# Decode attention: key pages turned in 32x32 blocks by VectorE and scored by TensorE in small tiles, values requested after the last gather

## The chip, the cores and the metric

One Trainium2 chip, one core of it. The metric is the device time of one launch in microseconds (us). The kernel before was run three times: 1145.11, 1141.04 and 1144.10 us, median 1144.1 us.

## What is computed

One layer of a decoder with a prompt group (256 tokens) and a sample group: 8 samples with 8 new tokens each and 2,048 past tokens in pages of 128. Cut to what the change touches, per sample:

```python
# MoBA: 8 heads, keys and values in paged cache [k, v]; top 3 blocks of 256 keys by mean key, plus the own block
gate = einsum('bthd,bnhd->bthn', q, kmean);  _, top = top_k(gate, 3)
# NSA: 8 query heads on 2 key heads; cache rows [k_cmp, v_cmp, k_sel, v_sel]
ck = gelu(flat(k_cmp) @ w1 + b1) @ w2 + b2        # 127 compressed keys, 32 rows each, stride 16; the same for v_cmp
p_cmp = softmax(q @ ck.T);  imp = p_cmp @ overlap  # importance of 64-row blocks
_, idx = top_k(imp, 16)                            # selected blocks, attended over k_sel, v_sel
o_win = attention over the last 512 rows (k_win, v_win)
```

All of it is float32. Ahead of the samples stand the input projections and the prompt's attention, behind them the mixers' projections and the feed-forward layer.

## The kernel before, in words

Four blocks follow each other: `front_block`, `prompt_block`, `decode_block` and `back_block`. The samples are done in `decode_block`: a prologue for sample 0, then a loop of 7 passes, in which the engines finish sample `it` while the segments of sample `it + 1` are prepared, and the last sample apart. In the trace the passes of the loop begin at 288.7, 348.8, 408.9 us and so on, the last sample at 708.9 us, and the back at 751 us. The order of each engine's work is written by hand (`sequence` of each engine); the PSUM banks that pass data from TensorE to VectorE and ScalarE are taken in turn from a ring of four (`RING`, the list `STEADY` of jobs), and TensorE may fill a bank when the job four places ahead in the list has been emptied (`wait_emptied`, L1162).

TensorE's pass (`sequence`, L1345) has two parts.

- From the key scores to the selected probabilities. `key_transposes` (L1225) turns the key pages of a quarter (4 of the 16 pages of 128 rows x 512) with 16 transposes of 128x128; ScalarE and VectorE copy each full bank to `KTr` (`key_copy`, L1491). `key_scores` (L1234) multiplies a quarter: 4 matmuls of 32 query columns by 512 keys. VectorE takes each quarter with a sum, a masked add and a maximum (`take_keys`, L1679). Between them stand `hidden_values` (L1261), 48 products of 128x128x128 for the compressed values, the own, window and compressed scores, and the importance (L1371). VectorE ranks the blocks (L1724 to L1745) and ScalarE takes the exponential of the selected scores (L1544); only then TensorE transposes the selected probabilities (job `psel`, L1386), the first job that needs them.
- From the probabilities to the next sample's segments. `segments(q)` transposes the compressed rows of a quarter that ScalarE has relaid (`relay_quarter`, L1521); `moba_values` (L1268) multiplies probabilities and values; `selected_transposes` (L1185) turns the selected keys and `selected_scores` (L1192) multiplies them for two quarters (a pair); `hidden_keys` (L1210) makes 12 products per quarter for the compressed keys; `compressed_values` (L1325), `compressed_products` (L1335) and `final_transposes` (L1293) finish sample `it`.

The NSA rows of a quarter come by an indirect DMA of POOL (`gather_segments`, L551) into one of two slots; `slot_free` (L1147) waits for the slot's copies and for the selected transposes of that quarter:

```python
pool.wait_ge(filled, nth(b - 1 if b else None, ("sel", q, 0)))
```

SyncE (`sequence`, L1107) requests key and value pages. Kr holds 8 key pages, so two quarters of keys are requested in the first part of the pass, and two for the next sample behind them. The next sample's values are requested as soon as `moba_values` has used a slot:

```python
for q in (1, 2, 0):
    sp.wait_ge(v_used, it * 4 + (q + 1 if q else 4))
    load_v(it + 1, q)
```

`prompt_block` begins on SyncE with 8 loads of the prompt's own NSA rows (L608).

## Time and profile before

| what | us |
|---|---|
| three runs, median | 1144.1 |
| profiled execution, its span (the page gives no other time of it) | 1140.6 |
| one pass of the loop (408.9 to 468.9 us) | 60.0 |
| TensorE busy over the span | 1051.8 |
| VectorE busy over the span | 528.8 |
| ScalarE busy over the span | 544.4 |

The page's busy time is an average over blocks with different limits. The change touches the decode loop, so that one pass of it is read: 408 to 468 us, the third of seven passes of the same length. Idle time of an engine stands in brackets before an instruction, with what ended it.

### The profile page before, as it was taken

Reading aid. Unit: us, or ns where it says so; the run is one execution under the profiler, and the core shown is the slowest. Engines: PE = TensorE matmul, PEld = TensorE weight load, DVE = VectorE, ACT = ScalarE, POOL = GpSimd, SP = SyncE. Lnnn points to the kernel's source line nnn. Section 1 sums busy time; section 2 is a strip of 40 time slices with the busy share of each in tenths; the row PEclk is TensorE's granted clock in tenths of the full one; section 3 lists DMA queues with packets and bytes.
Section 4 is the critical chain, followed back from the end, with each engine's and each line's share of the span. In section 5 each row is a group of like instructions: output and inputs, shape, how many; then the busy total and the mean of one; then the engine's idle time right before and its main releaser. Section 6 shows DMA issues by size and latency. Waiting matters only on the chain. (4 is left out here: it accounts for less than half of the span.)

```text
span 1140.6 us, 25588 instructions
## 1 busy us (share of the span) xinstructions
PE 1051.8 (92%) x9297; PEld 912.2 (80%) x9297; DVE 528.8 (46%) x1174; ACT 544.4 (48%) x1069; POOL 83.0 (7%) x59
## 2 busy tenths in 40 slices
PE   7789996867999999999999999989999799999997
PEld 3578874656777787778787878769998799999997
DVE  1500015524545545463637363657457755555324
ACT  3422214645575666565756564561543444443223
POOL 1143410001000000000000100000000000000000
PEclk9799995867999999999999999988999899999999
DMA  9797776407666575758484846593565154443501
GB/s 331 214 309 246 246 255 224 178 37 279 221 212 231 193 242 179 269 159 284 134 305 132 310 147 221 182 268 103 176 201 166 41 181 147 147 147 148 185 0 47
DMA packets 129909, 219.51 MB, mean 192 GB/s; under 512 B 19348, under 2 KB 74129, under 8 KB 125058
## 3 DMA queue, kind: packets, MB, share of 16 engines
q1 hardware_dynamic: 124962, 185.14, 49.2%
q0 software_dynamic: 4896, 33.68, 8.0%
q8 instruction: 34, 0.56, 0.2%
q14 instruction: 17, 0.14, 0.0%
HBM read 210.46 MB, written 12.45 MB: 195 GB/s over the span
## 5 line engine op out<-in xcount | busy, mean ns | idle before, releaser
L103 PE MATMUL ps<-b_uH,b_slabH 128*128 128x320 f32 x480 | 152.3, 317 | 8.8 <-DVE b_uL L2341 5.3
L104 PE MATMUL ps<-b_uL,b_slabH 128*128 128x320 f32 x480 | 151.7, 316 | 0.0
L105 PE MATMUL ps<-b_uH,b_slabL 128*128 128x320 f32 x480 | 151.0, 315 | 0.0
L1207 PE MATMUL ps<-t_XT,t_slab 128*128 128x128 f32 x1024 | 142.6, 279 | 4.6 <-DVE t_XT L1655 3.5
L2229 DVE TENSOR_TENSOR b_slabL<-t_slab,b_slabH 128x2048 fp32r<-128x2048 f32 (+1 forms) x52 | 109.3, 2124 | 65.2 <-ACT b_slabH L2122 65.2
L1207 PEld LDWEIGHTS ps<-t_XT,t_slab 128*128 128x128 f32 x1024 | 127.2, 193 | 14.8 <-issue 10.6
L2122 ACT ACTIVATE b_slabH<-t_slab 128x2048 fp32r<-128x2048 f32 (+1 forms) x52 | 92.3, 1783 | 96.0 <-PE ps L105 90.6
L103 PEld LDWEIGHTS ps<-b_uH,b_slabH 128*128 128x128 f32 x480 | 93.4, 195 | 10.3 <-issue 6.6
L1504 ACT ACTIVATE t_KTr<-ps 128x512 f32<-128x512 f32 x152 | 82.1, 592 | 23.4 <-PE ps L1231 19.9
L104 PEld LDWEIGHTS ps<-b_uL,b_slabH 128*128 128x128 f32 x480 | 93.3, 194 | 0.0
L105 PEld LDWEIGHTS ps<-b_uH,b_slabL 128*128 128x128 f32 x480 | 93.1, 194 | 0.0
L1207 PE MATMUL ps<-t_XT,t_taps 128*128 128x128 f32 x512 | 83.9, 279 | 0.0
L1231 PEld LDWEIGHTS ps<-t_ident,t_Kr 128*128 128x128 f32 x512 | 55.7, 141 | 20.1 <-issue 13.2
L1207 PEld LDWEIGHTS ps<-t_XT,t_taps 128*128 128x128 f32 x512 | 69.5, 192 | 2.1 <-issue 1.4
L551 POOL DMA_INDIRECT t_nsa<-cache_nsa_kv,t_index x32 | 30.1, 941 | 509.8 <-ACT t_vsel L1504 293.0
L1231 PE MATMUL ps<-t_ident,t_Kr 128*128 128x128 f32 x512 | 62.4, 275 | 0.1
L1654 DVE TENSOR_TENSOR t_XT<-ps,t_XT 128x256 f32<-128x256 f32 x64 | 26.9, 420 | 75.6 <-PE ps L1182 50.5
L1504 ACT ACTIVATE t_relay<-t_nsa 128x512 f32<-128x512 f32 x64 | 36.7, 620 | 38.1 <-DMA t_nsa<-cache_nsa_kv,t_index 37.9
L103 PE MATMUL ps<-b_GH,b_slabH 128*128 (+1 forms) x176 | 54.5, 310 | 0.0
L105 PE MATMUL ps<-b_GH,b_slabL 128*128 (+1 forms) x176 | 54.4, 309 | 0.0
L104 PE MATMUL ps<-b_GL,b_slabH 128*128 (+1 forms) x176 | 54.4, 309 | 0.0
L237 POOL TENSOR_TENSOR t_f_L<-t_slab,t_f_H 128x2048 fp32r<-128x2048 f32 x10 | 46.0, 4600 | 102.1 <-ACT t_f_H L418 102.1
(388 smaller groups left out, 2080.9 us busy)
## 6 DMA issues: line engine op xcount, KB each, us to landing
t_Kr<-cache_moba_kv SPq DMA_DIRECT2D x132, 256.0 KB, 3.0
t_Vr<-cache_moba_kv SPq DMA_DIRECT2D x124, 256.0 KB, 5.7
t_slab<-w_ada SPq DMA_DIRECT2D x22, 1024.0 KB, 7.9
t_slab<-w_gu SPq DMA_DIRECT2D x22, 1024.0 KB, 5.2
t_slab<-w_in SPq DMA_DIRECT2D x17, 1024.0 KB, 6.5
t_slab<-w_down SPq DMA_DIRECT2D x11, 1024.0 KB, 5.0
t_slab<-cmp_w SPq DMA_DIRECT2D x2, 2048.0 KB
t_wkv<-cache_nsa_win SPq DMA_DIRECT2D x8, 512.0 KB, 3.2
```

Of the source, the lines that this page charges most:

```text
L103: pe.matmul(out, w_high, x_high, start=start, stop=False, **kw)
L104: pe.matmul(out, w_high, x_low, start=False, stop=False, **kw)
L105: return pe.matmul(out, w_low, x_high, start=False, stop=stop, **kw)
L237: pool.tensor_tensor(slabL[j % 2][:, :], slab[:, j % 2, :], slabH[j % 2][:, :].bitcast(F32), ALU.subtract).then_inc(w_split, 1)
L551: pool.indirect_dma_start(out=t["nsa"][:, q % 2, :], out_offset=None, in_=d["cache_nsa_kv"], in_offset=bass.IndirectOffsetOnAxis(ap=t["ind ...
L1207: return pe.matmul(out[:, P * j:P * j + P], taps(w, j, lp)[:, P * ht:P * ht + P], XT[:, w, lp, j, :, :].rearrange("p v i -> p (v i)"), sta ...
L1231: last = pe.transpose(bank[:, P * j:P * j + P], Kr[:, 4 * (q % 2) + j, P * hp:P * hp + P], ident[:, :])
L1504: return act.activation(dst, src, ACT.Copy)
L1654: dve.tensor_tensor(XT[:, :, lp, 0, :, :], seg[:, :, :, 0:NSEG:2], odd, ALU.subtract)
L2122: act.activation(slabH[:, s, 0:values], slab[:, s, 0:values], ACT.Copy).then_inc(w_high, 1)
L2229: dve.tensor_tensor(slabL[:, s, 0:values], slab[:, s, 0:values], slabH[:, s, 0:values].bitcast(F32), ALU.subtract).then_inc(w_split, 1)
```

## The change

The MoBA keys are not transposed by TensorE any more. VectorE turns each key page in place, in blocks of 32x32 (`turn_keys`, 16 instructions of 128x512 per sample), and the selected keys too (`turn_selected`, 4 per sample). After that a block of 32 rows holds 32 head columns of 32 keys, so TensorE multiplies tiles of 32 rows by 32 columns: 128 matmuls of 256 columns for the key scores of a sample, in four row groups that go to four banks and four column groups, and 32 matmuls of 128 columns for each pair of selected quarters. The query tiles for it are copied once through DRAM (`spill_q`: 8 writes at the start of `prompt_block`, 4 reads per sample) and padded by ScalarE (`pad_queries`, 2 instructions). `take_keys` runs over the four banks, one row group each, and two small reductions join them, ahead of the MoBA ranking; `take_selected` takes four small pieces.

The copies to `KTr` are gone, and Kr holds all 16 pages: the next sample's 16 pages are requested at once behind this sample's key scores. The order of TensorE's pass changes, as below. ScalarE relays quarter 1 behind both gelu's. `slot_free` waits for the scores of a whole pair, so quarters 2 and 3 are gathered after the first pair's scores, and the next sample's quarters 0 and 1 after the second pair's. The next sample's value pages are requested only when the last quarter of that sample's NSA rows has landed. Some semaphores are shared, and the mask constants follow the new order of keys. `front_block` scales the queries with two VectorE instructions.

```diff
+            for n in range(2):
+                for r in range(4):
+                    sp.dma_start(d["spill_q"].rearrange("b (a n r x) -> a n r b x", a=32, n=2, r=4)[:, n, r, :, :],
+                                 t["q_out"][32 * r:32 * r + 32, n, :, :, :].rearrange("p b g t -> p b (g t)")).then_inc(t["q_spilled"], 16)
...
+NSA_JOBS = cmp_jobs(0) + cmp_jobs(1) + sel_jobs(0) + cmp_jobs(2) + cmp_jobs(3) + sel_jobs(1)
+FRONT_JOBS = ([("win", 0, 0)] + [("key", 0, i) for i in range(4)] + [("psel", 0, 0), ("psel", 1, 0), ("pwin", 0, 0)]
+STEADY = (FRONT_JOBS + cmp_jobs(0) + cmp_jobs(1) + [("values", 0, 0)] + sel_jobs(0) + [("cout", 0, 0)]
+          + cmp_jobs(2) + cmp_jobs(3) + [("final", 0, 0)] + sel_jobs(1))
...
             def sequence(it, more):
-                for q in range(2):
-                    sp.wait_ge(filled, nth(it, ("key", q, 3)))
-                    load_k(it, q + 2)
+                sp.wait_ge(filled, nth(it, ("key", 0, 3)))
                 if more:
-                    for q in range(2):
-                        sp.wait_ge(filled, nth(it, ("key", q + 2, 3)))
+                    load_queries(it + 1)
+                    for q in range(4):
                         load_k(it + 1, q)
                     sp.wait_ge(out_mm, it * N_OUT + 2)
                     load_window(it + 1)
-                if more:
                     sp.wait_ge(v_used, it * 4 + 1)
                     load_v(it, 3)
+                    sp.wait_ge(nsa_landed[1], it * 32 + 64)
+                    apart(sp, turns)
                     for q in (1, 2, 0):
                         sp.wait_ge(v_used, it * 4 + (q + 1 if q else 4))
                         load_v(it + 1, q)
...
-                pool.wait_ge(filled, nth(b - 1 if b else None, ("sel", q, 0)))
+                pool.wait_ge(filled, nth(b - 1 if b else None, ("sel", q // 2, 3)))
...
+                first = jobs.index(("sel", pair, 0))
+                    pe.wait_ge(taken, count)
+                    pe.wait_ge(q_landed, b * 64 + 64)
+                pe.wait_ge(sel_turned, b * 4 + (2 * pair + 2))
+                apart(pe, turns)
+                for db in range(2):
+                    for half in range(2):
+                        for kv in range(KV):
+                            r, c = 2 * kv + db, 64 * half + 32 * kv
+                            for i in range(4):
+                                rows32 = slice(32 * i, 32 * i + 32)
+                                last = pe.matmul(ps[RING[(first + i) % 4]][c:c + 32, 0:P].rearrange("p (l s) -> p l s", s=32),
+                                                 qsrc[rows32, P + 32 * r:P + 32 * r + 32],
+                                                 nsa[rows32, half, :].rearrange("p (l x) -> p l x", l=4)
+                                                 [:, :, 256 + 32 * r:256 + 32 * r + 32], start=db == 0, stop=db == 1)
+                last.then_inc(filled, 4)
...
-            def key_transposes(it, q):
-                for hp in range(4):
-                    bank = ring(it, ("key", q, hp))
-                    if hp == 0:
-                        pe.wait_ge(k_landed[q % 2], it * 128 + 64 * (q // 2 + 1))
-                    for j in range(4):
-                        last = pe.transpose(bank[:, P * j:P * j + P], Kr[:, 4 * (q % 2) + j, P * hp:P * hp + P], ident[:, :])
-                    last.then_inc(filled, 1)
-
-            def key_scores(it, q):
-
-                wait_emptied(it, ("key", q, 0))
-                wait_emptied(it, ("key", q, 3))
-                if q != 1:
-
-                    pe.wait_ge(scores_taken, it * N_SCORE + (AT_WIN + 1 if q == 0 else AT_KEYS + q - 1))
-                for hp in range(4):
-                    last = pe.matmul(ps[2 + q % 2][32 * hp:32 * hp + 32, :], qa[:, 32 * hp:32 * hp + 32],
-                                     KTr[:, 4 * (q % 2) + hp, :], start=True, stop=True)
-                last.then_inc(scored, 1)
+            def key_scores(it):
+
+                banks = [ring(it, ("key", 0, i)) for i in range(4)]
+                pe.wait_ge(q_staged, it * 6 + 6)
+                for n in range(2):
+                    pe.wait_ge(keys_turned, it * 16 + (8 * n + 8))
+                    apart(pe, turns)
+                    for r in range(4):
+                        for hp in range(4):
+                            for i in range(4):
+                                rows32, c = slice(32 * i, 32 * i + 32), 32 * (4 * hp + r)
+                                last = pe.matmul(banks[i][32 * hp:32 * hp + 32, 256 * n:256 * n + 256]
+                                                 .rearrange("p (g s) -> p g s", s=32),
+                                                 qk[rows32, r, hp, :], Kr[rows32, 8 * n:8 * n + 8, c:c + 32],
+                                                 start=r == 0, stop=r == 3)
+                last.then_inc(filled, 4)
...
+            def turn_selected(b, q):
+
+                dve.wait_ge(nsa_landed[q % 2], b * 32 + 16 * (q // 2 + 1))
+                keys = nsa[:, q % 2, :].rearrange("p (l x) -> p l x", l=4)[:, :, 256:384]
+                dve.transpose(keys, keys).then_inc(sel_turned, 1)
+
+            def turn_keys(b, pages):
+                for g in pages:
+                    if g % 8 == 0:
+                        dve.wait_ge(k_landed[g // 8], b * 128 + 128)
+                    dve.transpose(Kr[:, g, :], Kr[:, g, :]).then_inc(keys_turned, 1)```

Three places in the engines' order. TensorE, from the importance product (`t_Sc,t_c`) to the transposes of the selected probabilities (`t_ident,t_Ss`), before (the last sample's copy of the pass, which has the same order; `t_Kr` rows are key transposes, `t_KTr` rows key scores, `t_slab` and `t_taps` rows products of `hidden_values`):

```order
L1371 MATMUL ps<-t_Sc,t_c 128x127
L1242 MATMUL ps<-t_KTr,t_qa_cur 32x512 x4
L1231 MATMUL ps<-t_ident,t_Kr 128x128 x16
L1242 MATMUL ps<-t_KTr,t_qa_cur 32x512 x8
L1207 MATMUL ps<-t_XT,t_slab 128x128 x16
L1386 MATMUL ps<-t_ident,t_Ss 128x128 x8
```

and of the changed kernel, from the window scores (`t_XT,t_qb_cur`, 64x512) on:

```order
L1384 MATMUL ps<-t_XT,t_qb_cur 64x512
L1235 MATMUL ps<-t_XT,t_slab 128x128 x4
L1235 MATMUL ps<-t_XT,t_taps 128x128 x2
L1389 MATMUL ps<-t_ckT,t_qb_cur 64x127
L1235 MATMUL ps<-t_XT,t_taps 128x128 x6
L1235 MATMUL ps<-t_XT,t_slab 128x128 x6
L1396 MATMUL ps<-t_Sc,t_c 128x127
L1235 MATMUL ps<-t_XT,t_slab 128x128 x10
L1235 MATMUL ps<-t_XT,t_taps 128x128 x4
L1405 MATMUL ps<-t_ident,t_Ss 128x128 x8
```

All key scores now stand ahead of the first of these rows, with 12 products around them, and between the importance product and the selected probabilities 14 products stand where 16 transposes, 12 key score matmuls and 16 products stood.

TensorE in the second part of the changed kernel, from the compressed values to the segments of quarter 2 (`t_nsa,t_qsrc` are the first pair's selected scores, the two rows of L1235 come four times and are the 12 products of `hidden_keys(1)`, `t_Vr` is `moba_values(2)`, `t_relay` the first transposes of quarter 2's segments):

```order
L1355 MATMUL ps<-t_w,t_hid 127x64 x4
L1216 REGISTER_ALU x2
L1218 ISA
L1219 ISA
L1227 MATMUL ps<-t_nsa,t_qsrc 32x128 x32
L1186 REGISTER_ALU x3
L1235 MATMUL ps<-t_XT,t_slab 128x128 x2
L1235 MATMUL ps<-t_XT,t_taps 128x128
L1366 MATMUL ps<-t_cv,t_PTc 32x64 x2
L1304 MATMUL ps<-t_Vr,t_XT 32x128 x16
L1204 MATMUL ps<-t_ident,t_relay 128x128 x4
```

Between the first pair's scores, which free the slots of quarters 2 and 3, and the segments of quarter 2 stand 12 products, the compressed products and `moba_values(2)`. Before, the selected transposes of quarter 0 freed quarter 2's slot, far ahead.

VectorE in the same part of the changed kernel:

```order
L1811 TENSOR_TENSOR t_cv<-ps,t_b 127x128
L1679 STREAM_TRANSPOSE t_Kr<-t_Kr 128x512 x2
L1688 REGISTER_ALU
L1694 SCALAR_TENSOR_TENSOR t_Ss<-ps,t_cm 128x4x32 x4
L1697 REGISTER_ALU
L1698 TENSOR_REDUCE t_smax<-t_Ss 128x32
L1817 REGISTER_ALU
L1818 COPY t_On<-ps 64x64
L1679 STREAM_TRANSPOSE t_Kr<-t_Kr 128x512 x4
L1671 REGISTER_ALU
L1673 STREAM_TRANSPOSE t_nsa<-t_nsa 128x4x128
```

The key turns stand between the copies that TensorE waits for: the compressed values' copy (L1811) empties the bank ahead of the first pair's scores.

## Rows read from the trace of the kernel before

**Rows 1.** The page: the span, and busy time of each engine.

```profile
span 1140.6 us, 25588 instructions
PE 1051.8 (92%) x9297; PEld 912.2 (80%) x9297; DVE 528.8 (46%) x1174; ACT 544.4 (48%) x1069; POOL 83.0 (7%) x59
```

**Rows 2.** Windows of one pass: stretch, us, busy PE, PEld, DVE, ACT, POOL, clock, DMA share, GB/s.

```profile
407.85:433.04 25.19, 25.19 (x212) 19.01 (x211) 15.62 (x43) 14.23 (x28) 0.00 (x0) 1.00 0.64 211
433.04:442.77 9.73, 8.48 (x141) 6.94 (x141) 7.11 (x26) 8.65 (x32) 0.00 (x0) 1.00 0.36 114
442.77:467.85 25.08, 24.43 (x315) 21.29 (x314) 7.94 (x23) 14.93 (x28) 3.74 (x4) 1.00 0.79 270
407.85:467.85 60.00, 58.10 (x664) 47.24 (x664) 30.67 (x90) 37.80 (x88) 3.74 (x4) 1.00 0.66 220
```

**Rows 3.** Timeline of TensorE, first part: start, us, line, tiles, count of records.

```profile
408.86 1.96 PE L1231 MATMUL ps<-t_ident,t_Kr 128*128 128x128 f32 x16
...
418.32 1.07 PE L1361 MATMUL ps<-t_KTw,t_qb_cur 128*64 128x512 f32 x2
...
429.26 3.84 PE L1207 MATMUL ps<-t_XT,t_slab 128*128 128x128 f32 x32
```

**Rows 4.** Timeline of VectorE, then of ScalarE, in the first part.

```profile
422.57 0.68 DVE L1684 TENSOR_REDUCE t_gate<-ps 128x2 f32<-128x512 f32 x1
...
427.50 0.27 DVE L1724 TENSOR_REDUCE t_imp<-ps 128x30 f32<-128x120 f32 x1
...
431.69 1.20 ACT L1544 ACTIVATE t_Ss<-t_Ss,t_sstat 128x1088 f32<-128x1088 f32 x1 [3.55 <-DVE t_sstat L1745]
```

**Rows 5.** Timeline of TensorE, second part.

```profile
443.75 1.08 PE L1281 MATMUL ps<-t_Vr,t_KTr 128*32 128x128 f32 x32
...
451.24 0.66 PE L1189 MATMUL ps<-t_ident,t_nsa 128*128 128x128 f32 x4
...
456.75 1.08 PE L1201 MATMUL ps<-t_KTr,t_qb_cur 128*64 128x512 f32 x4
```

**Rows 6.** Timeline of the other engines, second part: gathers, relays, gelu, values' copy, value loads.

```profile
447.25 0.94 POOL L551 DMA_INDIRECT t_nsa<-cache_nsa_kv,t_index  x1 [41.73 <-ACT t_vsel L1504]
452.70 0.94 POOL L551 DMA_INDIRECT t_nsa<-cache_nsa_kv,t_index  x1 [4.52 <-PE ps L1189]
...
445.55 0.91 ACT L1540 ACTIVATE t_hid<-t_hid,t_hbias 128x256 f32<-128x256 f32 x2
453.77 1.15 ACT L1504 ACTIVATE t_relay<-t_nsa 128x512 f32<-128x512 f32 x2 [3.15 <-DMA t_nsa<-cache_nsa_kv,t_index]
...
449.36 0.29 DVE L1789 TENSOR_TENSOR t_cv<-ps,t_b 127x128 f32<-127x128 f32 x1 [4.03 <-PE ps L1331]
...
445.67 19.67 SPq L1093 DMA_DIRECT2D t_Vr<-cache_moba_kv  x16
```

**Rows 7.** Page, DMA queues: packets, MB, share; and a window of full DMA.

```profile
q0 software_dynamic: 4896, 33.68, 8.0%
...
280.78:286.38 5.60, 5.60 (x50) 5.50 (x51) 3.21 (x8) 3.43 (x6) 0.94 (x1) 1.00 1.03 396
```

**Rows 8.** Timeline of TensorE in the prompt's scores: two row tiles of 64.

```profile
202.36 2.00 PE L647 MATMUL ps<-t_ksT_p,t_qbT_p 64*128 64x256 f32 x16
```

**Rows 9.** TensorE's idle stretches in brackets, and windows behind them with the granted clock.

```profile
280.78 1.15 PE L1182 MATMUL ps<-t_ident,t_relay 128*128 128x128 f32 x8 [1.75 <-ACT t_relay L1504]
754.39 0.64 PE L103 MATMUL ps<-b_uH,b_slabH 128*128 128x320 f32 x1 [3.54 <-DVE b_uL L2247]
894.10 0.61 PE L103 MATMUL ps<-b_uH,b_slabH 128*128 128x320 f32 x1 [5.27 <-DVE b_uL L2341]
...
754.40:760.00 5.60, 5.60 (x21) 5.60 (x22) 5.60 (x6) 5.60 (x6) 0.00 (x0) 0.50 1.12 353
894.20:899.80 5.60, 5.60 (x21) 5.60 (x22) 5.42 (x18) 1.89 (x4) 0.00 (x0) 0.50 0.01 3
```

**Rows 10.** Timeline of SyncE's queue at the start of the prompt block.

```profile
174.23 5.21 SPq L608 DMA_DIRECT2D t_nsa<-nsa_kv_prompt  x8
```

More of the change, by code:

```diff
@@ L1261, in hidden_values @@
             def hidden_values(it, ht, steps, final):
-                out = ps[RING[jobs_of(it).index(("hidden", 1, 1)) % 4]] if ht else ps[6]
+                out = S_WIN if ht else S_OUT
                 for n in steps:
@@ L1477, in _ @@
             sequence(NB - 1, False)
-        def nsa_copy(eng, copy, it, job):
-            kind, q, i = job
-            bank = ps[RING[(NSA_JOBS if it is None else STEADY).index(job) % 4]]
-            eng.wait_ge(filled, nth(it, job))
-            return copy(KTr[:, q, :], bank[:, :])
         def segments(eng, it, q, i):
```

351 lines of the change are left out of this document (180 added, 171 removed).

## The prediction

> **What bounds the kernel now.** I read the page first: TensorE is busy for 92% of the 1140.6 us span, VectorE and ScalarE for under half [rows 1]. That is an average, so the windows of one pass come next [rows 2]. The pass takes 60.0 us and falls into three parts. Part A, from the second pair's selected scores to the selected probabilities, is 25.2 us with TensorE busy throughout. Part B, from there to the first segments, is 9.7 us, and TensorE is idle for 1.25 us of it behind ScalarE's exponentials. Part C, the next sample's segments, is 25.1 us with 0.65 us idle. So any work taken off TensorE shortens the pass, as long as no chain of the other engines is as long. The timelines show those chains: how late the exponential of the selected scores comes [rows 4], and how long a gather takes from POOL to ScalarE's relay [rows 6].
>
> **Part A.** Before, the window scores start 10.5 us into the part (407.85 to 418.32). Ahead of them the change removes the second pair's scores (1.0, now in part C), two groups of 16 key transposes (1.96 each [rows 3], 3.7 without their overlap) and 6 of 18 products. A product is 3.84 us over 16, 0.24 us [rows 3], so 1.4. It adds the whole key scores: 256 records of 256 columns, which by 16 tiles at once are 16 rounds. The nearest row has 8 rounds of 256 columns in two row tiles: 2.00 us, 0.25 each [rows 8]. That makes 4.0 us, if 16 tiles share as well as two. 10.5 - 1.0 - 3.7 - 1.4 + 4.0 = 8.4.
>
> From there the part hangs on VectorE and ScalarE. Window scores to the first key sum: 4.25 (418.32 to 422.57). Two `take_keys` (before, 422.57 to 427.50 with a copy and a wait among them) shrink to six operations of about 0.66, 3.95. The ranking is unchanged, 427.50 to 431.69 or 4.2, and the exponential until the probabilities, 431.69 to 433.04, 1.35 [rows 4]. Together 13.7, so the probabilities come at 22.1: a **gain of 3.1**. TensorE's own work would have allowed more: 8.4, the window scores 1.0, 32 products 7.7 and two small products of at most 1 make 18.1. TensorE therefore waits **4.0 us** for the exponential, where the 16 key transposes and 12 score matmuls were its cover. Of what the change takes from TensorE here, more than half becomes this wait.
>
> **Part B** keeps its operations. Two small reductions join the chain of VectorE, at most 0.27 each as the smallest row of that kind [rows 4]: **+0.5**, 10.2.
>
> **Part C.** Work first: four transposes of selected keys go (0.66, 0.6 without overlap [rows 5], 2.4) and the first pair's scores of 1.0. Two pairs in small tiles come: 64 records of 128 columns are 4 rounds, and a round of 128 columns is 1.08 over 8, 0.135 [rows 5], so 0.55 each. The 0.65 idle goes too. 25.1 - 2.4 - 1.0 + 1.1 - 0.65 = 22.2. Then the new waits:
>
> - Relay of quarter 1 now stands behind both gelu's. Those start 2.8 us into the part and take 0.91, half a relay is 0.57 [rows 6]: 4.3, while TensorE wants quarter 1 after segments and two `moba_values`, 3.1. **1.2**.
> - The first pair's scores wait until VectorE has emptied the compressed values' bank, 0.29 and the hand-overs, 0.3 to 0.8, taken as **0.55**.
> - Quarter 2's gather starts only when the first pair's scores are done. POOL started 0.8 us behind TensorE's transposes before (451.90 to 452.70 [rows 5, 6]). From POOL's start to the relay it was 6.5 us, with value loads alongside on SyncE's queue [rows 6]; those now wait. From below: 33.68 MB over 32 gathers are 1.05 MB, at the 396 GB/s of a full stretch 2.7 us [rows 7], and POOL's 0.94, so 3.6. I take 5.6, nearer to the measured row than to the bound. With 0.8 and 0.57 that is 7.0. TensorE has 12 products, the compressed products and `moba_values(2)` to do, 2.9 + 0.2 + 1.0 = 4.1. Wait **2.9**, with ends 0.9 and 3.8. What is late behind it is everything up to the next sample's first product, since TensorE works in order.
> - Quarter 3 lands 2.7 us behind quarter 2, against segments, `moba_values(3)` and own values, 2.3: **0.3**.
> - The second pair's scores wait for the final copy, which on VectorE stands behind three turned pages: **0.9**, ends 0.2 and 1.5.
>
> Sum 5.85, so part C is 28.0.
>
> **VectorE** gets 20 turns of 128x512 per pass. The trace has no such operation. A reduction of this size takes 0.68 [rows 4], so I take 0.65 and 13 us; VectorE is busy for 7.9 us in part C [rows 2] and has room to 28. Hidden, but for the final copy above. From below nothing changes if they are quicker; from above see the third rival. ScalarE only loses the copies.
>
> The pass is 22.1 + 10.2 + 28.0 = **60.3**, 0.3 longer, although TensorE's work in it falls by about 10 us.
>
> **The clock.** Behind idle stretches of TensorE of 3.54 and 5.27 us the granted clock is 0.50, that is 1.2 instead of 2.4 GHz, for at least 5.6 us; behind one of 1.75 us it is 1.00 [rows 9]. The pass now has stretches of 4.0 and 2.9 us. Half speed over 5.6 us costs 2.8 us of work. The first is followed by part B, whose 1.25 us of idle and 0.5 of added wait take up most: 1.05. The second is followed by full work, where the lateness covers quarter 3 and half of the final copy: 2.0. Together **+3.0**, so **63.3** per pass.
>
> **Sum.** Seven passes by 3.3: +23.1. The last sample has parts A and B alone: -3.1 + 0.5 + 1.0 = -1.6. The prologue turns all 16 pages before the first hidden sum, 10.4 us of VectorE, mostly beside gathers and TensorE's products: +2, ends -2 and +10. The spill puts 8 writes of 0.65 (5.21 over 8 [rows 10]) ahead of the prompt's segment loads: +1, ends 0 and 5.2. Eight writes of queries and their reads move too little to count, and the next sample's pages, requested early, have most of a pass to land. 23.1 - 1.6 + 3 = +24.5, from 1140.6 to 1165.1. The profiled execution lies 3.5 us below the median of the runs, so the forecast is **1169 us**. Own range: 1154 (first clock fall alone) to 1190.
>
> **Rivals.**
>
> 1. **The clock stays up** (0.26). Waits are broken into pieces of under 2 us, by scattered small work. Then the pass is 60.3, the sum +2.1 - 2.6 + 3 = 2.5, and the time **1147**; 0.14 of this lies within 0.5%, 0.12 above. For it: idle of 1.75 us had no effect. Against: both waits hang on a single event each.
> 2. **TensorE remains the bound: faster** (0.24). If quarter 2 is at its relay 3.6 us after POOL's start and the smaller waits of part C vanish into that lateness, C is 22.2 + 0.9 = 23.1. With the first clock fall the pass is 22.1 + 10.2 + 23.1 + 1.0 = 56.4, the sum 7 x (-3.6) + 1.4 = -23.8, the time **1120**. It decides when waits in C and the clock cost less than 5.5 us a pass together. For it: the value loads, which shared the DMA engines with the gather, are put off. Against: POOL to relay in 6.5 us.
> 3. **VectorE becomes the bound** (0.05). If a turn costs 1.3 us, twice the reduction, VectorE needs 7.9 + 26 = 33.9 in part C; pass 22.1 + 10.2 + 33.9 + 1.0 = 67.2, time **1196**. For it: no row shows a block turn. Against: every operation of this size takes 0.6 to 0.75. The Trainium skill ("VectorE: DVE Perf Modes", The three transpose paths) gives 311 ns for 128x128 in bf16, and four of those would be an estimated 1.24 us per page, which is this case; no trace here shows it.
> 4. **Small tiles do not run side by side in rows** (0.04). If only four column groups share, key scores take 64 rounds, 16 us, and each pair 2.2: +12 and +3.2, pass 78.5, last sample +12, time **1287**. Against: two row tiles of 64 do share [rows 8]. The Trainium skill ("TensorE: Matmul & The Clock Gate", Measured speedup vs the span model) states 10.6 times for 16 tiles, not 16. By that the key scores would be an estimated 6.0 us and the time 1185, which the range holds.
> 5. **Putting off the value loads does nothing** (0.03): the gather stays at 6.5, +0.9 a pass, **1175**.
>
> **How the numbers follow.** My forecast has 0.38. A measurement of this kernel can tell 0.5% from no change, 1138.4 to 1149.8. Faster: rival 2, 0.24. Same: 0.14 of rival 1. Slower: 0.38 + 0.12 + 0.05 + 0.04 + 0.03 = 0.62. The range reaches down to 1117, so as to take in more than half of rival 2, and up to 1192, where the forecast with its upper bounds ends; rivals 3 and 4 and the rest of 2 are left out, some 0.2.
>
> **What would show it.** Right: TensorE's transposes of the selected probabilities wait 4 us for the exponential; segments of quarter 2 wait some 3 us for the relay, and that for the gather; granted clock under 1.00 in the loop; turns of 0.65 us; key scores of 4 us. Wrong: clock 1.00 throughout with passes of 60 (rival 1), TensorE busy through part C with passes under 58 (rival 2), turns over 1 us, or key scores over 6 us.

## The result, and the profile after it

The changed kernel takes **1254.35 us** (median of 1256.03, 1251.72, 1258.40 and 1252.66) against 1144.61 for the kernel before on the same chip (1145.11, 1141.04, 1144.1, 1145.68). The ratio is 1.0968, with a 95% interval of 1.0939 to 1.0998: slower by almost 10%. The direction was forecast (0.62 for slower). The size was not: 1254 lies above the range of 1117 to 1192.

The page of the changed kernel, its first lines, the granted clock, the queue of instruction fetches and two groups:

```profile
span 1254.2 us, 29746 instructions
PE 1049.7 (84%) x11409; PEld 921.2 (73%) x11409; DVE 623.5 (50%) x1377; ACT 476.0 (38%) x949; POOL 83.0 (7%) x59
...
PEclk9789977668898998889887897897799989999999
...
q8 instruction: 98, 1.61, 0.5%
...
L1679 DVE STREAM_TRANSPOSE t_Kr<-t_Kr 128x512 f32<-128x512 f32 x128 | 80.1, 675 | 0.0
L1263 PE MATMUL ps<-t_Kr,t_qk 32*32 32x256 f32 x2048 | 58.3, 487 | 27.6 <-issue 27.5
```

Beside [rows 1], TensorE is busy for the same time (1049.7 against 1051.8 us) with 2112 more records, and its share falls from 92% to 84%: 113.6 us were added to the span, nearly all of it idle. VectorE gained 95 us, ScalarE lost 68. The block turn costs 675 ns, as taken (0.65). The last row holds what the forecast had no term for. Ahead of the small-tile key scores TensorE idles for 27.5 us, put down to "issue": nothing that the profile shows was waited for. And the queue of instructions has 98 packets of 16 KB. The same line of the page of the kernel before is in the second fence below.

The passes start at 300.25, 372.44, 448.24, 523.57, 598.69, 674.13, 748.99 and 821.71 us (first product of L1374 each time), 74.49 us apart on average, against 60.16 before (L1355). The third is taken apart here. Windows of the changed kernel: the whole pass, then the way from the hidden sums ahead of the pass to the selected probabilities, and from there to the first segments. Behind them stand the key scores and three stretches of low clock:

```profile
448.24:523.57 75.33, 56.55 (x926) 47.21 (x927) 42.37 (x115) 29.12 (x73) 3.75 (x4) 0.91 0.53 176
442.71:478.52 35.81, 23.78 (x398) 19.59 (x398) 15.70 (x46) 7.67 (x15) 1.87 (x2) 0.94 0.54 184
478.52:489.86 11.34, 10.21 (x133) 8.26 (x133) 7.51 (x28) 8.95 (x34) 0.00 (x0) 0.74 0.63 206
454.29:462.49 8.20, 7.00 (x257) 5.06 (x257) 0.00 (x0) 0.00 (x0) 0.00 (x0) 0.83 0.06 22
453.60:457.00 3.40, 2.71 (x91) 2.00 (x98) 0.00 (x0) 0.00 (x0) 0.00 (x0) 0.50 0.31 117
477.50:484.30 6.80, 5.78 (x47) 5.05 (x51) 5.54 (x18) 4.46 (x15) 0.00 (x0) 0.50 0.68 214
508.20:511.60 3.40, 3.40 (x47) 2.31 (x45) 2.38 (x6) 2.44 (x7) 0.00 (x0) 0.50 0.22 92
```

In [rows 2] a pass had 58.10 us of busy TensorE at a clock of 1.00. Now it has 56.55 us, part of it at 0.50, and 18.8 us of idle. Queue lines of the transfers in one pass (packets, MB, share), first of the kernel before (408.86 to 468.85), then of the changed one (448.24 to 523.57):

```profile
q1 hardware_dynamic: 4799, 9.00, 46.2%
q0 software_dynamic: 576, 4.20, 19.3%
q14 instruction: 1, 0.01, 0.0%
```

```profile
q8 instruction: 10, 0.16, 0.9%
```

Before, nothing of queue 8 falls into this pass, nor into the other passes behind the first, which has six packets; the whole page has 34. After, every pass brings nine or ten. Where TensorE stands still shows in its timeline of that pass:

```profile
448.24 0.65 PE L1374 MATMUL ps<-t_ident,t_wkv 128*128 128x128 f32 x4 [2.85 <-issue]
...
454.29 6.38 PE L1263 MATMUL ps<-t_Kr,t_qk 32*32 32x256 f32 x253 [3.61 <-issue]
461.87 0.62 PE L1263 MATMUL ps<-t_Kr,t_qk 32*32 32x256 f32 x3 [1.20 <-issue]
...
478.52 1.97 PE L1405 MATMUL ps<-t_ident,t_Ss 128*128 128x128 f32 x8 [4.37 <-ACT t_Ss L1556]
...
494.12 1.18 PE L1204 MATMUL ps<-t_ident,t_relay 128*128 128x128 f32 x8 [1.33 <-ACT t_relay L1506]
...
499.73 1.06 PE L1227 MATMUL ps<-t_nsa,t_qsrc 32*32 32x128 f32 x64 [0.76 <-DVE t_cv L1811]
...
507.79 1.64 PE L1204 MATMUL ps<-t_ident,t_relay 128*128 128x128 f32 x8 [3.00 <-ACT t_relay L1506]
...
517.01 1.06 PE L1227 MATMUL ps<-t_nsa,t_qsrc 32*32 32x128 f32 x64 [0.77 <-DVE t_oT_s L1848]
```

Two families of idle. The waits of the forecast are all there and at their size: exponential 4.37 (4.0), relay of quarter 1 1.33 (1.2), copy of the compressed values 0.76 (0.55), relay of quarter 2 3.00 (2.9), final copy 0.77 (0.9). Ahead of them stand three waits on issue, 2.85 + 3.61 + 1.20 = 7.66 us, at the start of the pass and in the key scores. Behind the second the clock is at 0.50 (453.60 to 457.00), and the key scores, busy for 4.47 us in experiment 4, which has no such stalls and half the records, are busy for 7.00. The gather and the relay of quarter 2, timeline of POOL and ScalarE:

```profile
501.59 0.94 POOL L555 DMA_INDIRECT t_nsa<-cache_nsa_kv,t_index  x1 [56.18 <-PE ps L1227]
...
507.11 1.15 ACT L1506 ACTIVATE t_relay<-t_nsa 128x512 f32<-128x512 f32 x2 [10.87 <-DMA t_nsa<-cache_nsa_kv,t_index]
```

That is 5.52 us from POOL to the relay, 5.6 in the forecast and 6.5 in [rows 6].

**Theory A**: TensorE's loop has become too long for the store that holds an engine's instructions, so its code is fetched again in every pass, and TensorE stands still where many short instructions stand together. Counted from the program, with two instructions for a matmul and four for one whose rows are two records, the body of TensorE's loop goes from about 1400 to about 1910 instructions, that is from 5.5 to 7.5 packets of 256 (experiment 4 bears the 256 out). The Trainium skill ("Runtime: NRT & Kernel Launch", Instruction fetch mechanics) says that the store is refilled in blocks of 16 KB, 256 instructions, holds 2048 on TensorE, and that a taken branch whose target is not in its window of two blocks forces a fetch. The packets of 16 KB agree. The loop before, which branches back over some 1400 instructions in six passes without a packet, does not agree with a window of two blocks, and a loop of 1910 that does not stay is not what 2048 would suggest. **A first rival**: small tiles are slow to issue in themselves, and the code's fetches merely stand beside that. **A second**: the waits of the forecast and the clock behind them account for the loss. The expectations word the rivals anew for each run.

### The profile page after: what moved, and what is told of

Same layout as the page of the kernel before. It is cut to its first block and busy times, and to the rows that moved or that the text cites. A ratio compares the mean times of both kernels' runs of the same rounds, so it can differ in the third digit from the quotient of the medians.

```text
span 1254.2 us, 29746 instructions
## 1 busy us (share of the span) xinstructions
PE 1049.7 (84%) x11409; PEld 921.2 (73%) x11409; DVE 623.5 (50%) x1377; ACT 476.0 (38%) x949; POOL 83.0 (7%) x59
## 3 DMA queue, kind: packets, MB, share of 16 engines
q0 software_dynamic: 4896, 33.68, 7.3%
q8 instruction: 98, 1.61, 0.5%
## 5 line engine op out<-in xcount | busy, mean ns | idle before, releaser
L103 PE MATMUL ps<-b_uH,b_slabH 128*128 128x320 f32 x480 | 152.3, 317 | 8.8 <-DVE b_uL L2375 5.3
L1235 PE MATMUL ps<-t_XT,t_slab 128*128 128x128 f32 x1024 | 149.6, 284 | 0.1
L1235 PEld LDWEIGHTS ps<-t_XT,t_slab 128*128 128x128 f32 x1024 | 131.0, 196 | 15.2 <-issue 13.8
L103 PEld LDWEIGHTS ps<-b_uH,b_slabH 128*128 128x128 f32 x480 | 93.1, 194 | 10.3 <-issue 6.6
L1235 PE MATMUL ps<-t_XT,t_taps 128*128 128x128 f32 x512 | 93.3, 300 | 0.0
L1263 PE MATMUL ps<-t_Kr,t_qk 32*32 32x256 f32 x2048 | 58.3, 487 | 27.6 <-issue 27.5
L1679 DVE STREAM_TRANSPOSE t_Kr<-t_Kr 128x512 f32<-128x512 f32 x128 | 80.1, 675 | 0.0
L1235 PEld LDWEIGHTS ps<-t_XT,t_taps 128*128 128x128 f32 x512 | 77.5, 211 | 2.7 <-issue 2.7
L1204 PE MATMUL ps<-t_ident,t_relay 128*128 128x128 f32 x256 | 43.0, 320 | 40.0 <-ACT t_relay L1506 40.0
L1263 PEld LDWEIGHTS ps<-t_Kr,t_qk 32*32 32x32 f32 x2048 | 41.2, 118 | 42.4 <-issue 35.6
L1506 ACT ACTIVATE t_relay<-t_nsa 128x512 f32<-128x512 f32 x64 | 36.6, 618 | 91.9 <-DMA t_nsa<-cache_nsa_kv,t_index 91.9
L555 POOL DMA_INDIRECT t_nsa<-cache_nsa_kv,t_index x32 | 30.0, 939 | 619.3 <-PE ps L1227 572.6
L1204 PEld LDWEIGHTS ps<-t_ident,t_relay 128*128 128x128 f32 x256 | 33.2, 163 | 48.4 <-ACT t_relay L1506 41.9
L103 PE MATMUL ps<-b_GH,b_slabH 128*128 (+1 forms) x176 | 54.6, 310 | 0.0
```

The source lines that it names most:

```text
L103: pe.matmul(out, w_high, x_high, start=start, stop=False, **kw)
L555: pool.indirect_dma_start(out=t["nsa"][:, q % 2, :], out_offset=None, in_=d["cache_nsa_kv"], in_offset=bass.IndirectOffsetOnAxis(ap=t["ind ...
L1204: last = pe.transpose(bank[:, P * c:P * c + P], relay[:, i, P * c:P * c + P], ident[:, :])
L1235: return pe.matmul(out[:, P * j:P * j + P], taps(w, j, lp)[:, P * ht:P * ht + P], XT[:, w, lp, j, :, :].rearrange("p v i -> p (v i)"), sta ...
L1263: last = pe.matmul(banks[i][32 * hp:32 * hp + 32, 256 * n:256 * n + 256] .rearrange("p (g s) -> p g s", s=32), qk[rows32, r, hp, :], Kr[ro ...
L1506: return act.activation(dst, src, ACT.Copy)
```

## The experiments

### 1. The key scores in 64 wide products instead of 128

```diff
-                for n in range(2):
-                    pe.wait_ge(keys_turned, it * 16 + (8 * n + 8))
+                pe.wait_ge(keys_turned, it * 16 + 16)
...
-                        qk[rows32, r, hp, :], Kr[rows32, 8 * n:8 * n + 8, c:c + 32],
+                        qk[rows32, r, hp, :], Kr[rows32, :, c:c + 32],
```

> The changed kernel with its key scores as 64 matmuls of 512 columns instead of 128 of 256: the same columns in half the instructions. Theory A (TensorE's loop no longer stays in its instruction store, so that each pass fetches it again: 98 instruction packets on the page instead of 34, nine of them in each pass of 74.5 us, and 7.7 us of idle 'issue' at the pass's start and in the key scores): some 256 instructions less bring the loop back, the packets in the loop vanish, the issue idle falls under 1 us a pass and the granted-clock fall behind it goes; pass 64 to 66 us, time 1175 to 1195 us. Rival B (the issue idle is a wait for turned keys or queries that the profile does not name): idle and pass stay, 1240 to 1260 us. Rival C (the small tiles themselves are slow, and issue idle is TensorE's limit on small instructions): the idle inside the key scores halves, that at the start stays, 1215 to 1240 us.

Measured: 1237.77 us (1233.03 to 1244.25), ratio 1.0831 [1.0782, 1.0881]; passes of 72.06 us. The waits on issue of this run, and its queue of instructions:

```profile
PE ps L1262 <- issue: 16.6, 7, 3.5
PE ps L1371 <- issue: 16.2, 6, 3.1
```

```profile
q8 instruction: 90, 1.47, 0.5%
```

The body is shorter by some 240 instructions, yet the fetches go on, eight to nine a pass, and with them both stalls. So the time that A expected of a loop that fits did not come. By its numbers this run is close to rival C: 1237.77 lies in C's range, the idle at the key scores falls from 27.5 to 16.6 us and that at the pass's start stays (15.3 before, 16.2 now). Experiments 4 and 5 decide between A and C. What the page says for A is that the loop still did not stay. By the count its 6.5 packets still lay across eight, as it begins and ends in the middle of one. Whether that is the reason is what experiment 5 asks.

### 2. TensorE's passes written out one after the other

```diff
-            with pe.Fori(0, NB - 1) as it:
+            for it in range(NB - 1):
                 sequence(it, True)
```

> The changed kernel with TensorE's seven passes written out one after the other instead of a loop; the other engines keep their loops, and every matmul stays. Theory A, if code that is read straight on is fetched ahead of its use: no idle at a pass's start, and the pass falls to 64 to 68 us, 1175 to 1205 us, though the packets stay at nine a pass. If fetching cannot keep up with 512 instructions in the 4 us of the key scores, part of the idle there remains, 1205 to 1230 us. Rivals B and C: 1240 to 1260 us, since waits and tiles are the same.

Measured: 1228.88 us, one run; passes of 71.33. The stall at the start of a pass is gone in all seven. The one in the key scores stayed, as this row of TensorE's timeline shows:

```profile
450.96 2.53 PE L1263 MATMUL ps<-t_Kr,t_qk 32*32 32x256 f32 x104 [3.48 <-issue]
...
513.11 4.68 PE L1263 MATMUL ps<-t_Kr,t_qk 32*32 32x256 f32 x229
```

No branch is taken here, so the stall in the key scores is not the loop's alone. 256 records, some 512 instructions or two packets, are used up there within an estimated 5.2 us of work (229 take 4.68 us in the second row, ahead of their stall). Around the first stall packets came 3.4 and 4.2 us apart (448.65, 452.09, 456.26), in the pass of the section on the result 3.6 to 4.1 (451.54, 455.33, 459.42, 463.06). Passes written out alone leave the stall in the key scores; wide key scores alone left both.

### 3. The kernel before with a longer loop

50, and in another run 150, small products of 8 columns per sample. They write a corner of a bank that nothing reads.

```diff
+                for _ in range(50):
+                    pe.matmul(ps[7][0:64, 128:136], qb[:, :], t["kwT_s"][:, 0:8], start=True, stop=True)
                 pe.matmul(ps[7][0:64, 128:192], qb[:, :], t["kwT_s"][:, :], start=True, stop=True).then_inc(small_mm, 1)
```

> The kernel before with 50 small matmuls of 8 columns (64 rows, 64 query columns) ahead of the last of the own scores in each sample, whose output the last one overwrites: some 200 instructions more in the loop. Theory A: the loop still fits, no instruction packets in the passes, and the time rises by the work alone, 1.5 to 4 us a sample, 1156 to 1176 us.

> The same with 150 of them, some 600 instructions more, about the changed kernel's loop. Theory A: instruction packets appear in every pass, TensorE has over 2 us of issue idle at the start of each pass, and the time rises by clearly more than three times the rise with 50, some 1190 to 1250 us. Rivals B and C: no idle at the pass's start, the rise is three times that with 50.

Measured: 1230.86 with 50 and 1435.38 with 150, one run each. Both are far above what was expected, because of the products. With 50, their row in TensorE's timeline of one pass, and windows at their start and near their end:

```profile
438.56 8.05 PE L1260 MATMUL ps<-t_kwT_s,t_qb_cur 128*64 128x8 f32 x100
```

```profile
438.56:441.00 2.44, 2.44 (x45) 2.44 (x44) 0.00 (x0) 0.08 (x1) 0.00 (x0) 1.00 0.62 201
444.00:446.60 2.60, 2.60 (x26) 2.60 (x26) 0.00 (x0) 0.00 (x0) 0.00 (x0) 0.50 0.00 0
```

That is 8 us a sample, where 1.5 to 4 were expected. The clock falls from 1.00 to 0.50 in the middle of them, though TensorE has no gap there, and is still at 0.50 behind them (446.60 to 452.00); the kernel before has no fall in its loop. As a price of time the pair is spoiled. What they still tell apart is the fetching: 36 packets with 50 (34 without), 93 with 150, and only with 150 this idle, in its waits:

```profile
PE ps L1231 <- issue: 25.3, 6, 5.0
```

It is 4.2 us at the start of each pass but the first, in a kernel with no small-tile scores. A longer loop alone brings it on, in this kernel between some 1600 and some 2000 instructions: for A, against the first rival.

### 4. Wide key scores and passes written out, together

The edits of experiments 1 and 2.

> Both edits together: TensorE's passes written out, and the key scores as 64 matmuls of 512 columns. The written-out kernel has passes of 69.0 us (442.3 to 511.2), with one stop of 3.5 us in the key scores and a fall of the granted clock behind it. Theory A (these stops are code arriving late; half as many instructions in the same time let it arrive): no stop over 1 us in the key scores, pass 63 to 65 us, which is the forecast's 63.3, time 1180 to 1200 us. Rival C (the stop belongs to the small tiles): the stop stays, 1220 to 1230 us.

Measured: **1185.06 us** (1184.47 to 1186.6), ratio 1.0355 [1.0302, 1.0407]; passes of 65.21 us. No product of TensorE waits on issue for more than 0.5 us any more. Windows of one pass: to the selected probabilities from the hidden sums on, to the first segments, and the whole pass; then its timeline of TensorE:

```profile
429.72:455.72 26.00, 21.45 (x275) 16.98 (x270) 15.86 (x46) 7.67 (x15) 1.87 (x2) 0.98 0.79 266
455.72:467.12 11.40, 10.12 (x132) 8.35 (x133) 7.57 (x28) 8.95 (x34) 0.00 (x0) 0.74 0.62 192
...
432.50:497.77 65.27, 53.64 (x800) 44.36 (x799) 42.35 (x116) 29.14 (x73) 3.75 (x5) 0.92 0.61 204
455.72:461.30 5.58, 5.58 (x40) 4.83 (x44) 4.58 (x17) 3.37 (x13) 0.00 (x0) 0.50 0.73 212
```

```profile
434.82 4.47 PE L1262 MATMUL ps<-t_Kr,t_qk 32*32 32x512 f32 x128
...
455.72 1.97 PE L1402 MATMUL ps<-t_ident,t_Ss 128*128 128x128 f32 x8 [4.29 <-ACT t_Ss L1553]
...
484.96 1.59 PE L1204 MATMUL ps<-t_ident,t_relay 128*128 128x128 f32 x8 [3.32 <-ACT t_relay L1503]
```

The computation and its order between the engines are those of the changed kernel, only TensorE's code differs: 1254.35 - 1185.06 = **69 us were the code**, its stalls and the falls of the clock behind them. Up to an estimated 6 us of this can be the halved number of records itself, 5.2 - 4.47 = 0.7 in each of eight samples. The page has 74 packets where experiment 2 has 82: eight less for 64 matmuls of four instructions less in each of eight samples, so a packet holds 256. The rest, 40.6 us over the kernel before (1144.46 on this chip), is what the second rival can claim. The small tiles are quick when their code is there: 4.47 us for the whole key scores. The first rival falls, and with it rival B of experiment 1, since the waits for turned keys and queries are still there.

### 5. The loop kept, its code moved by 172 instructions

Experiment 1 with 43 small products once ahead of the loop, into a bank that is not in use, so that by the count the loop lies across seven packets instead of eight.

```diff
             pe.wait_ge(om_taken, 1)
+            for _ in range(43):
+                pe.matmul(ps[4][0:64, 0:8], ident[:, 0:64], ident[:, 0:8], start=True, stop=True)
             with pe.Fori(0, NB - 1) as it:
```

> The loop is kept, with the key scores of 512 columns, and 43 small matmuls stand once ahead of the loop, so that the loop's code begins 172 instructions later. Counting two instructions for a transpose and four for a float32 matmul, the loop of the run with 512 columns is 6.5 blocks of 256 instructions long, but lies across 8 of them, and 90 packets came; with the shift it begins near a block's border and lies across 7, as the kernel before's does. Theory A in this form: 36 to 40 packets, no issue idle at the pass's start, pass 63 to 66 us, 1180 to 1205 us. If the number of blocks is not what decides, or the count is off: 90 packets and 1230 to 1242 us.

Measured: 1212.4 us (1208.9 to 1215.45), ratio 1.0601 [1.0546, 1.0657]: between the two outcomes. Its page has 55 instruction packets against 90. The passes take 70.5, 67.2, 65.3, 65.4, 65.0, 69.4 and 67.1 us. The queues of the transfers from 436.7 to 640 us, all that there are:

```profile
q1 hardware_dynamic: 15799, 28.91, 44.5%
q0 software_dynamic: 1728, 12.58, 16.6%
q14 instruction: 1, 0.01, 0.0%
```

Packets come in the first two passes, and again from 705.0 on, at the start of the seventh, which a wait on issue of 4.22 us puts off to 709.46 (it is in the 69.4); none comes between 436.6 and 705.0. The three passes from 444.42 to 640.1 take 65.2 us on average, as in experiment 4; with the same loop body experiment 1 had 72.06. Waits on issue at the start of a pass fall from six to two, those ahead of the key scores from seven to none. So where the loop's code lies decides whether it stays, as far as one trace shows it. Why it is fetched twice before it does, and once more for the last pass, is open.

### 6. The kernel before with its passes written out

> The kernel before with TensorE's seven passes written out one after the other instead of a loop; the work and its order stay. What it tells: whether straight-line code costs something of its own, so that the runs with TensorE's passes written out (1185 us for the changed kernel) still contain a price of code. Theory A (a pass of some 1400 TensorE instructions, spread over 60 us, is fetched in time when its code is straight): 1139 to 1155 us, no idle on issue over 0.3 us in the seven passes, and some 70 packets on the instruction queue instead of 34. Rival (code that is not kept from pass to pass always costs idle of TensorE): stalls on issue of 2 us or more in each pass where many small matmuls stand together, 1160 us or more.

Measured: 1144.84 us (1141.41 to 1148.43), ratio 1.0007 [0.9983, 1.0032]. The edit is that of experiment 2.

```profile
q8 instruction: 66, 1.08, 0.4%
```

32 packets more for six more copies of the body, 5.3 each; by the count 5.5. The time is the same. In the traced execution, which took 1148.43 us, the passes are 61.49 us apart against 60.16 before, but no wait of TensorE on issue is above 0.4 us. Code that is fetched in every pass is no loss by itself: it is one when a branch goes back to code that is gone, or when more short instructions stand together than the fetch brings in time. As a side result, the 69 us of experiment 4 hold no price of straight code for this kernel.

### 7. Values requested early again

Experiment 4 without the wait of the next sample's value loads on the last rows:

```diff
                     load_v(it, 3)
-                    sp.wait_ge(nsa_landed[1], it * 32 + 64)
-                    apart(sp, turns)
                     for q in (1, 2, 0):
```

> The written-out kernel with 512 columns, and the next sample's values requested as before, as soon as a slot is free, without waiting for the last rows. The forecast's step: POOL's start to the relay goes from 5.5 to about 6.5 us, quarter 2 is that much later, the pass 0.5 to 0.9 us longer, 4 to 7 us more than the same kernel with the wait. Rival: the wait does nothing, within 2 us of it. Other rival: the wait costs, since values come late: 2 to 6 us less.

Measured: 1207.84 us (1200.59 to 1210.3), 22.8 above experiment 4; passes of 68.11. Timeline of POOL and ScalarE:

```profile
488.98 0.94 POOL L555 DMA_INDIRECT t_nsa<-cache_nsa_kv,t_index  x1 [45.22 <-PE ps L1225]
...
496.63 1.15 ACT L1501 ACTIVATE t_relay<-t_nsa 128x512 f32<-128x512 f32 x2 [12.55 <-DMA t_nsa<-cache_nsa_kv,t_index]
```

From POOL to the relay it is now 7.65 us instead of 5.73 in experiment 4 (478.46 to 484.19). In that stretch 306 packets of the value loads' queue run beside the gather's 224, where experiment 4 has none. TensorE's wait for quarter 2 grows from 3.32 to 5.24. So this part of the change is worth 23 us, more than the 4 to 7 expected. The 6.5 us of [rows 6], from which they were expected, held one gather with the loads: POOL started the next one 5.5 us later. Here it starts it 1.2 us later (490.22). That this is why 7.65 came instead of 6.5 is not shown.

### 8. Orders that fill the waits

Three versions on top of experiment 4. The first moves the key scores behind four products, the two key sums on VectorE ahead of the own scores, the first pair's scores ahead of the compressed values, and two blocks of MoBA values ahead of quarter 2's segments:

```diff
-                hidden_values(it, 0, range(0, 8), False)
+                hidden_values(it, 0, range(0, 4), False)
                 key_scores(it)
...
-                segments(2)
                 moba_values(it, 3)
                 moba_own_values(it)
+                segments(2)
```

> The written-out kernel with 512 columns and both waits of the forecast attacked. First part: key scores behind 4 products instead of 8, and VectorE takes the first two key banks ahead of the own scores, where it is idle, instead of ahead of the ranking. Second part: the first pair's scores ahead of the compressed values, and moba_values(3) and the own values ahead of the segments of quarter 2. Theory (the two waits of TensorE and the clock falls behind them are the price of the change, once code comes in time): the wait for the exponential falls from 4.4 to under 1.5 us, that for quarter 2 from 3.0 to under 1, the values' copy no longer stops TensorE, and the clock stays at 1.00 there; 7 to 9 us a pass less, 1125 to 1150 us, faster than the kernel before if it meets the lower half. Rival (VectorE's chain to the MoBA probabilities sets the pass, so the waits move behind it): 2 to 4 us a pass less, 1160 to 1180 us.

Measured: 1170.84 us (1167.77 to 1174.67), ratio 1.0236 [1.0178, 1.0294], passes of 62.78. TensorE's timeline:

```profile
449.80 1.09 PE L1400 MATMUL ps<-t_ident,t_Ss 128*128 128x128 f32 x8 [2.26 <-ACT t_Ss L1551]
456.70 0.63 PE L1337 MATMUL ps<-t_ident,t_XT 128*128 128x128 f32 x4 [1.83 <-ACT t_XT L1551]
...
476.45 1.15 PE L1204 MATMUL ps<-t_ident,t_relay 128*128 128x128 f32 x8 [1.01 <-ACT t_relay L1501]
480.34 1.94 PE L1204 MATMUL ps<-t_ident,t_relay 128*128 128x128 f32 x8 [2.75 <-ACT t_relay L1501]
```

The exponential's wait goes from 4.29 to 2.26 and quarter 2's from 3.32 to 1.01, but 1.83 and 2.75 appear behind them, at the MoBA exponentials and at quarter 3. The theory's 1125 to 1150 us are missed; time and pass are those of the rival. The next version moves a part of the hidden sums between the segments, more turns to earlier places on VectorE, and the spill behind the prompt's loads:

```diff
-                segments(3)
                 hidden_keys(it, it + 1, 2)
+                segments(3)
                 final_transposes(it)
```

> The run before with passes of 61.5 us, and what its trace still showed idle: key scores first of all products, the turned pages spread over VectorE's idle stretches so that they are ready; the importance product straight behind the compressed scores' probabilities; half of hidden_keys(0) ahead of the segments of quarter 1 (1.4 us of wait), hidden_keys(2) between the segments of quarters 2 and 3 (2.75 us of wait); in the prologue half of the key turns earlier, and the spill of the queries behind the prompt's loads. Theory (each of these waits belongs to the order of the work, and none to the amount): some 1.5 us less in the first two parts, 3.5 in the third, no fall of the clock in the pass, 55 to 57.5 us a pass, 5 to 9 us less ahead of the loop, 1120 to 1140 us, faster than the kernel before. Rival (VectorE's chain takes the place of each wait removed): 59 to 60.5 us a pass, 1150 to 1165 us.

Measured: 1165.0 us (1164.91 to 1168.13), ratio 1.019 [1.0158, 1.0222], passes of 63.01: a miss by 25 us. The passes are no shorter than 62.78, and longer than the rival's 59 to 60.5 too.

```profile
444.63 1.09 PE L1398 MATMUL ps<-t_ident,t_Ss 128*128 128x128 f32 x8 [0.92 <-ACT t_Ss L1550]
...
473.92 0.68 PE L1235 MATMUL ps<-t_XT,t_slab 128*128 128x128 f32 x4 [1.80 <-DVE t_XT L1648]
...
480.76 1.06 PE L1227 MATMUL ps<-t_nsa,t_qsrc 32*32 32x128 f32 x64 [2.33 <-DVE t_oT_s L1842]
```

What the exponential gave, VectorE's copies took: quarter 2's differences 1.80, the final copy 2.33. The last version brings the final transposes and their copy ahead of quarter 2's segments, lets ScalarE scale the output before it relays quarter 2, and splits a hidden sum around quarter 3:

```diff
                 moba_own_values(it)
+                final_transposes(it)
                 segments(2)
-                hidden_keys(it, it + 1, 2)
+                hidden_keys(it, it + 1, 2, (0,))
                 segments(3)
-                final_transposes(it)
+                hidden_keys(it, it + 1, 2, (1,))
```

> The run before had passes of 61.5 to 66.7 us (mean 63.0): two waits went, and two came in their place, 2.3 us for the final copy, which stands on VectorE behind quarter 3's segments and two turned pages, and 1.8 us for the copies of quarter 2's segments. Here the final transposes and their copy stand ahead of quarter 2's segments, where TensorE waits for the gather anyway, ScalarE scales the output before it relays quarter 2, hidden_keys(2) is split around the segments of quarter 3, and three products stand again ahead of the key scores (0.8 us of wait there). Theory (order alone): 3 to 4 us of idle less a pass and fewer falls of the clock, 57.5 to 59.5 us a pass, 1125 to 1145 us. Rival (the gather of quarter 3 sets the end of the pass whatever stands around it): 61 to 62.5 us, 1150 to 1163 us.

Measured: **1134.21 us** (1127.53 to 1139.45), ratio 0.9909 [0.9873, 0.9945], passes of 58.29: faster than the kernel before, by a little under 1%. Its page:

```profile
PE 999.0 (88%) x10385; PEld 879.7 (78%) x10385; DVE 622.5 (55%) x1377; ACT 477.8 (42%) x949; POOL 83.0 (7%) x59
...
q8 instruction: 74, 1.21, 0.4%
```

TensorE is busy for 53 us less than in [rows 1], which is what the change takes off it once its code does not stand in the way, stretches at half clock counted in; about 10 us of that remain as a gain. The expectation was met. The mean granted clock of the seven passes is 0.96, against 0.91 in experiment 4 and 1.00 in the kernel before. The longest waits left in a pass are 1.84 at the MoBA exponentials and 1.81 at quarter 2's differences.

## Why the prediction was wrong in size and right in its waits

The step that failed is the sum itself, where it says "The pass is 22.1 + 10.2 + 28.0 = 60.3" and adds the clock: every term is work or a wait for data, and none is TensorE's code, which was put at nothing without a reason. The text priced the 256 records of the key scores by columns ("16 rounds") and no rival asked how 500 more instructions in the loop get to the engine. The 34 packets on the page of the kernel before, and the number of records that each pass gains, would have allowed the question. The runs put this at 69 us of the 85 by which 1254 exceeds 1169 (experiment 4; up to 6 of them can be the number of records). That fetching follows the loop's length is shown by experiment 3, that it follows the place of its code by experiment 5, and that fetching without a stall costs nothing by experiment 6. The other 16 us are sizes. Point by point, each pass from its first product of the window's keys (L1374, L1371):

| us | forecast | experiment 4, 432.50 on | changed kernel, 448.24 on |
|---|---|---|---|
| part A to the window scores | 8.4 | 9.40 | 16.38 |
| from there to the probabilities | 13.7 | 13.82 | 13.90 |
| part B, clock included | 11.25 | 11.40 | 11.34 |
| part C, clock included | 30.0 | 30.65 | 33.71 |
| pass | 63.3 | 65.27 | 75.33 |

- **Part A.** The key scores take 4.47 instead of 4.0 (16 tiles share nearly as well as two); 0.5 more lies in the products around them. The chain of VectorE and ScalarE held: 13.82 against 13.7, and so did the wait for the exponential, 4.29 against 4.0. In the changed kernel the part is 7 us longer: 3.61 and 1.20 on issue and 7.00 - 4.47 = 2.5 of key scores, in twice the records and part of them at half clock, with 0.4 less behind them.
- **Part B** held, with the clock at 0.50 from 455.72 to 461.30.
- **Part C** held: its four waits in experiment 4 are 1.42, 0.48, 3.32 and 0.58, 5.8 together against 5.85; the fifth, 0.3 for quarter 3, did not come. In the changed kernel the idle before the next pass, 2.62, comes on top, and half of the remaining 0.4 is the slower final copy.
- **Clock.** Right: 0.50 behind the waits of 4.4 and 3.0 us, 1.00 behind the shorter ones. The second fall lasts 3.4 us where the forecast took 5.6 from [rows 9]. Not foreseen was a third fall, behind the stall on issue. The length of the wait does not settle it: behind the 3.48 us of experiment 2 the clock is at 1.00 (450.96 to 456.00).
- **VectorE.** 0.675 a turn against 0.65, hidden as forecast. Rival 3 (1.3 us) falls. The Trainium skill ("VectorE: DVE Perf Modes", The three transpose paths) led to an estimated 1.24 us per page; the trace does not agree.
- **Small tiles.** Rival 4 falls, and so do the 6.0 us estimated from the Trainium skill ("TensorE: Matmul & The Clock Gate", Measured speedup vs the span model).
- **Ends.** The loop starts at 300.25 (300.89 in experiment 4) where the comparable start before was 288.70: +12, forecast +3, ends to +10 and +5.2. About 4 us of it are there by the prompt block (its transposes of the scores start at 242.94 instead of 238.80): the prompt's loads start at 178.38 instead of 174.23 [rows 10], behind the spill, which was priced at 1. The rest comes with the gathers ahead of the loop, where quarter 2's relay keeps TensorE waiting for 3.19. The turns, 9.60 us in a row, lie mostly beside that.
- **Values.** Rival 5 priced the putting off at 0.9 a pass. It is worth 2.9 (68.11 - 65.21); the longer wait for quarter 2 is 1.9 of it in the pass shown.
- **Sum.** In experiment 4 passes give 7 x 5.05 = 35.4 (forecast 23.1), the start 12.2 (3) and the last sample with the end -4.4 (-1.6): 43.2 against 24.5.
- Rivals 1 and 2, in which the pass gets shorter or stays, had the wrong conditions for this order, since the waits were real. Rival 2's mechanism is what the last version of experiment 8 reaches by another order.

The timeline of SyncE's queue in the changed kernel that "Ends" reads, the spill and the prompt's loads behind it:

```profile
174.55 3.78 SPq L609 DMA_DIRECT2D spill_q<-t_q_out  x8
178.38 5.21 SPq L616 DMA_DIRECT2D t_nsa<-nsa_kv_prompt  x8
```

## What to carry to other kernels

Where few large products become many small ones, count the instructions of each engine's loop body beside the columns, and read the queue of instruction fetches on the page: no packets in a pass means that the loop stays, packets in every pass with idle on issue mean that it doesn't. Then use the widest free size and, if needed, write the passes out. And work that is taken off an engine which also served as cover for a chain elsewhere returns as waits until the order is made anew: here the order alone was worth 51 us (1185.06 to 1134.21).

## What the runs showed of the hardware that was not expected

- A TensorE loop of some 1670 instructions was fetched again in every pass (90 packets on its page, 72.06 us a pass) or stayed for three whole passes (no packet, 65.2 us) depending on 172 instructions ahead of it.
- A stall on issue also occurs without a branch, 3.48 us where 256 small records stand together. The clock was at 1.00 behind this one, and at 0.50 behind the 3.61 us of the changed kernel.
- 100 records of products of 8 columns with 128 rows, one after the other, took 8.05 us, and the granted clock fell from 1.00 to 0.50 while they ran without a gap, so they are no free filler.
- From the start of a gather of 1 MB to the relay that reads it passed 5.5 to 5.7 us without direct loads beside it and 7.65 with them, at a DMA share of 0.71 to 0.72 and 0.89; the next gather ran behind it in both.
